# Last pair's third and second-layer expert matrices in four transfers each, with a wait per quarter on TensorE

## The chip, the cores and the metric

The kernel runs on one core of a Trainium2 chip. The metric is the device time of one execution in microseconds (us). One inference step of a small two-layer model for 512 prompt rows and 8 sample rows (one new token each) is one execution.

## The reference

Each of the two layers ends in a mixture of experts over all 520 rows. Cut to what matters here:

```python
yb = silu(xb @ w1[e]) * (xb @ w3[e])   # w1, w3: 1024 x 512, float32
yb = yb @ w2[e]                        # w2: 512 x 1024, float32
y  = sum over a row's two experts of gate * yb
x  = x + y
```

A row is routed to 2 of 32 experts. The matrices of all 32 experts are used in each layer, 3 x 2 MB per expert, so 201 MB per layer are read from HBM whatever the routing says. After layer 0 comes the mixer of layer 1 (means over windows of 2 to 16 rows, then four 256 x 256 maps), after layer 1 the final RMSNorm.

## The kernel before, in words

Everything is float32. Before the experts of layer 0 stand the projections, the attention and the recurrence (the first 400 us or so). The experts of a layer `l` are done in 16 pairs (`PAIRS`): the columns of TensorE are split in two halves of 64 (`CAP`), one expert of the pair in each, so that a pair takes three pair matrices of 4 MB: w1, w3 and w2.

**Slots.** `ring` has six pieces of 16 KB per partition, two per slot; slot 0 is for w1, slot 1 for w3, slot 2 for w2 from pair 4 on (before that four slots rotate). SyncE (SP) issues all weight transfers in one order on one queue: `load(l, i, j, slot, before)` waits until the matrix that lay in the slot has been used (`w1_used`, `h_done`, `y_done`), and issues one transfer that signals `wt_in[slot]`. So a slot's next matrix is requested when PE is done with the last one.

**One pair on PE** (`pair`): wait for w1, `products(0)`; wait for w3, `products(1)` (line 2221, the trace lists 32 matmul records per matrix, in the order of `k`, 0 to 7); transposes of the next pair's rows (`turn`); ACT and DVE form `silu(a) * b` (lines 1187 and 1768); four transposes of it (line 2427), a copy by DVE (line 1773); wait for w2, `results` (line 2247), whose outer loop is over the two 512-column blocks; ACT scales the sum (line 1193) into `yst`, and POOL scatters its rows into `y_rows` in HBM.

**The last pair of a layer** (`last=True`) differs before already. Its w2 comes in two transfers (line 766) with signals `wt_in[2]` and `wt_in[3]`, and `results_by_half` (line 2236) takes `k` as the outer loop and waits for the second half in its middle. Its rows are not scattered. Behind the two transfers SP waits for `w1_used` and for the scatter of pair 14, and then issues `load_results`: for each of the five row tiles (128 rows each, the last has 8) one transfer that gathers the other experts' results from `y_rows` (line 721). For the tiles 0, 1 and 2 DVE adds both gathered parts to `x` (`combine`, lines 1554 and 1557). PE then turns the last pair's rows back to their tokens (`rows_of_last`, lines 2465 and 2466, tile by tile), and DVE adds that (`add_last`, line 1567). Of one thing the order matters here: `rows_of_last(3)` waits until DVE has done `add_last` of tile 0, and `rows_of_last(4)` until that of tile 1, since they take the same PSUM banks. In layer 1 a part of the gathered rows of tiles 3 and 4 is added by PE (line 2465) instead of DVE.

DVE has the order `combine` 0, 1, 2, `add_last` 0 and then, in layer 0, `add_last` 1, the norm of tile 0 for the mixer of layer 1 (lines 1254 and 1255), `add_last` 2, `combine` 3; in layer 1 `combine` 3 and `add_last` 1. Behind `rows_of_last` of layer 0 PE begins the mixer (`mix`, line 2189, and `maps`, line 2210); behind that of layer 1 only norms and stores are left.

`QUARTER` is 1024 words of each of a partition's two 4096-word pieces: two values of `k` in w3, one in w2. The w3 of pair 1 comes in such quarters before the change too (line 754).

Of the kernel before, what the change touches and what calls it, by code (L numbers as in the profile page):

```python
# [7 lines left out]
ALU = mybir.AluOpType  # L24
# [105 lines left out]
def build(nc, a, outs, consts):  # L130
# [11 lines left out]
    with ExitStack() as ctx:  # L142
# [206 lines left out]
        eps_ready = sem("eps_ready")  # L349
# [8 lines left out]
        pick_ready = sem("pick_ready")  # L358
# [7 lines left out]
        rel_ready = sem("rel_ready")  # L366
        brow_done = sem("brow_done")
        brow_ready = sem("brow_ready")
# [19 lines left out]
        SELF_OUT, LOGITS_OUT, PROBS_OUT, PROBS_T_OUT, HEADS_OUT = 1, 2, 3, 5, 7  # L388

        sample_step = sem("sample_step")  # L390
        QUERIES, LOGITS, PROBS_TURNED, ATTENDED, GATES_TURNED, HEADS_TURNED = range(1, 7)
# [4 lines left out]
        lbl_ready = sem("lbl_ready")  # L396
# [23 lines left out]
        s_read = sem("s_read")  # L420
        snorm_ready = sem("snorm_ready")
        osq_summed = sem("osq_summed")
# [9 lines left out]
        late_clear = sem("late_clear")  # L432
# [5 lines left out]
        wr_ready = sem("wr_ready")  # L438
# [17 lines left out]
        hn_stored = [sem(f"hn_stored{l}") for l in range(2)]  # L456
# [15 lines left out]
        wt_in = [sem(f"wt_in{j}") for j in range(4)]  # L472
        w1_used = sem("w1_used")
# [107 lines left out]
        def landed(l, i, j, turned):  # L581

            n = 3 * i + j
            slot = slot_at(i, j) if turned else j
            if slot == 3:
                return 32 * (3 * l + n // 4 + 1) + 16 * l
            in_quarters = 48 * (l + (not turned or n >= 4)) if slot == 0 else 0
            return 16 * ((PAIRS - 1) * l + (n // 4 + 1 if turned else i)) + in_quarters
# [31 lines left out]
        def _(sp):  # L620
# [34 lines left out]
            sp.wait_ge(brow_ready, 2)  # L655
# [67 lines left out]
            for l in range(2):  # L723
# [73 lines left out]
        def _(pool):  # L797
# [10 lines left out]
            pool.wait_ge(brow_ready, 1)  # L808
# [32 lines left out]
            for l in range(2):  # L841
                for p, t in enumerate(TILE_ORDER[l]):
                    n = rows_of(t)
                    pool.wait_ge(hn_ready, TILES * l + p + 1)
                    pool.dma_start(hn_rows[l][t * P:t * P + n, :], hall[0:n, t, :]).then_inc(hn_stored[l], 16)
                pool.wait_ge(hn_stored[l], 16 * TILES)
# [48 lines left out]
        def _(act):  # L895
# [15 lines left out]
            def evacuate(unit, half=0):  # L911
# [14 lines left out]
                elif m == NT:  # L926
                    if PICKED[c]:
                        act.wait_ge(part_picked, PICKED[c])
                    act.wait_ge(pick_ready, 1)
# [4 lines left out]
            act.wait_ge(eps_ready, 1)  # L934
# [16 lines left out]
            act.wait_ge(lbl_ready, 1)  # L951
# [35 lines left out]
            def state_decayed(b):  # L987
                if b == 0:
                    act.wait_ge(s_read, 1)
# [121 lines left out]
            def experts(l):  # L1111
# [30 lines left out]
                if l == 0:  # L1142
                    late = TILE_ORDER[0].index(NT)
                    for u in range(TILES + 1):
# [3 lines left out]
                        if u == late:  # L1148
                            act.wait_ge(wo_done, 2 * u + 2)
                            act.wait_ge(late_clear, 1)  # L1150
# [94 lines left out]
        def _(dve):  # L1245
# [11 lines left out]
            V.memset(eps, EPS).then_inc(eps_ready, 1)  # L1257
# [11 lines left out]
            V.tensor_tensor(lbl, lbl, wide(lbs, [P, 2, HEADS], 1), ALU.subtract).then_inc(lbl_ready, 1)  # L1269

            dve.wait_ge(rel_in, 32)
            V.memset(relx[BUCKETS:BUCKETS + 1, :], 1.0).then_inc(rel_ready, 1)
            dve.wait_ge(rel_ready, 1)
            V.tensor_copy(relrep[0:BUCKETS + 1], wide(relx[0:BUCKETS + 1, :], [BUCKETS + 1, NB, HEADS], 1)).then_inc(rel_ready, 1)
            dve.wait_ge(consts_in, 16)
            V.tensor_reduce(pick, ident.rearrange("p (g c) -> p c g", g=4)[:, 32 - NB:32, :], AX.X, ALU.add).then_inc(pick_ready, 1)
            dve.wait_ge(brow_done, 1)
            V.tensor_copy(brow[0:HEADS], ps[0:HEADS, 4:6, :].rearrange("p a b -> p (a b)")[:, 0:ROWW]).then_inc(brow_ready, 1)
            V.tensor_copy(dbias[0:32], ps[0:32, 6, 0:NDEC]).then_inc(brow_ready, 1)
# [131 lines left out]
            def sample_heads():  # L1411

                dve.wait_ge(s_read, 1)
# [5 lines left out]
            def sample_means():  # L1419
                dve.wait_ge(osq_summed, 1)  # L1420
# [107 lines left out]
            V.memset(partial_late, 0.0).then_inc(late_clear, 1)  # L1528
# [10 lines left out]
            def sample_attended():  # L1539
                dve.wait_ge(sample_step, ATTENDED)  # L1540
                V.tensor_copy(dheads, ps[:, 1, :]).then_inc(decode_step, 2)
# [52 lines left out]
            def experts(l):  # L1594
# [74 lines left out]
                if l == 0:  # L1669
                    for u in range(TILES + 3):  # L1670
# [3 lines left out]
                        if u == 1:  # L1674
# [3 lines left out]
                                            wide(gain_of_router.rearrange("p l k -> p (l k)"), [P, 2 * KC, NG + NE], 2), ALU.mult).then_inc(wr_ready, 1)  # L1678
# [96 lines left out]
                dve.wait_ge(hn_stored[l], 16 * TILES)  # L1775
# [86 lines left out]
        def _(pe):  # L1862
# [41 lines left out]
            def pick_samples(c):  # L1904

                pe.wait_ge(piece_out, upto(UNIT[c, NT]))
                if c == IB:
                    pe.wait_ge(pick_ready, 1)
# [97 lines left out]
            def sample_states(part):  # L2006
# [7 lines left out]
                if part == 3:  # L2014
                    for h in range(HEADS):
                        T.transpose(ps[:, 5, 32 + h * NB:32 + (h + 1) * NB], ib[0:NB, NT, h * DH:(h + 1) * DH], ident[0:NB, 0:NB])
                    T.matmul(ps[:, 5, 64:96], ones, qk.rearrange("p h b -> p (h b)"), start=True, stop=True).then_inc(s_read, 1)

            def sample_squares():
                pe.wait_ge(snorm_ready, 1)  # L2020
                T.matmul(ps[:, 5, 96:128], ones, osq.rearrange("p h b -> p (h b)"), start=True, stop=True).then_inc(osq_summed, 1)
# [62 lines left out]
            for u in range(UNITS):  # L2084
# [7 lines left out]
                elif u == NT:  # L2092
                    pe.wait_ge(rel_ready, 2)
# [3 lines left out]
                    T.matmul(ps[0:32, 6, 0:NDEC], relrep[0:BUCKETS + 1].rearrange("p b h -> p (b h)"), onehot[0:BUCKETS + 1, ROWW:],  # L2097
                             start=True, stop=True).then_inc(brow_done, 1)
                for c in (IB, VA):
                    if u == PICK_AT[c]:  # L2100
                        if c == IB:
                            pe.wait_ge(brow_ready, 2)
# [111 lines left out]
            def products(j, pieces, by_quarter=False):  # L2214
# [3 lines left out]
                for k in range(KC):  # L2218
                    for half, w in enumerate(mats):
# [328 lines left out]
```

## Time and profile before

| what | value |
|---|---|
| time before, median of 3 runs | 1472.81 us (1470.75 to 1473.42) |
| the profiled execution: its span, first to last instruction | 1470.9 us |
| a time of its own beside the span | none is given for it |
| PE matmul busy | 1266.4 us, 86% of the span |
| DVE, ACT, POOL busy | 358.8, 247.0, 83.9 us |
| HBM traffic | 479.75 MB read, 36.56 MB written, 351 GB/s over the span |
| mean granted TensorE clock | 0.952 of full |
| the last pair's products with w3, layer 0 and layer 1, begin at | 875.78 and 1427.58 us |
| the last pair's results, layer 0 and layer 1, begin at | 887.56 and 1439.37 us |

The median stands 1.9 us above the span of the profiled execution. A line such as `L2221` is line 2221 of the kernel before. PE is the matmul side of TensorE, SPq the part of SyncE that issues transfers; in a transfer row the size is that of one transfer and the time is from issue to landing, that is until all of it is there and its signal is complete. The kernel after has the same code some 20 lines higher up.

### The profile page before, as it was taken

The page shows a single profiled execution, that of the slowest core. Times are in us where ns is not written, and L with a number is a line of the kernel's source. Part 1 is how long each engine was busy: PE and PEld are TensorE (multiplying, and loading weights), DVE is VectorE, ACT ScalarE, POOL GpSimd, SP SyncE. Part 2 cuts the span into 40 slices and gives each one's busy share as a digit, 9 for nine tenths or more (in the row PEclk, how much of TensorE's full clock was granted, in tenths as well). Part 3 has the DMA queues.
Part 4 walks back from the last instruction along what each step waited for, and adds up shares of the span by engine and source line. Part 5 has one row for each costly group of instructions (what it writes and reads, how often), then busy time and mean ns, then how long its engine had stood idle before and what let it go on. Part 6 is the DMA issues. An engine that isn't in the chain of part 4 may idle for free.

```text
span 1470.9 us, 14537 instructions
## 1 busy us (share of the span) xinstructions
PE 1266.4 (86%) x5864; PEld 613.9 (42%) x5864; DVE 358.8 (24%) x826; ACT 247.0 (17%) x440; POOL 83.9 (6%) x101
## 2 busy tenths in 40 slices
PE   7999999999999877878878798999977867778787
PEld 3688965644543322322322235853322322322232
DVE  2055487522431000010100007541010000100006
ACT  3243643342200000000000003410000000000002
POOL 1000000000000110000000000000000000000000
PEclk9999999999999988899999999989999999999998
DMA  9435766327479999999999998469999999999994
GB/s 347 103 78 174 219 175 215 106 80 316 201 277 427 426 402 421 427 427 426 428 425 427 426 419 345 194 231 418 426 426 429 426 429 427 427 426 424 428 414 164
DMA packets 75918, 492.94 MB, mean 335 GB/s; under 512 B 16813, under 2 KB 21581, under 8 KB 50774
## 3 DMA queue, kind: packets, MB, share of 16 engines
q1 hardware_dynamic: 59440, 449.35, 74.9%
q0 software_dynamic: 13568, 37.03, 7.5%
q10 hardware_dynamic: 2862, 5.91, 1.2%
q8 instruction: 31, 0.51, 0.1%
q14 instruction: 17, 0.14, 0.0%
HBM read 479.75 MB, written 36.56 MB: 351 GB/s over the span
## 4 chain that ended last, share of the span: by engine, by line
PE 51%; DMA 40%; DVE 5%; ACT 2%; issue 2%; ACTq 0%; SPq 0%; DVEq 0%
DMA ring<-in_moe_w 39%; PE ps L2221 20%; PE ps L1899 5%; PE ps L1892 4%; PE ps L2151 3%; PE ps L2247 3%; PE ps L2321 1%; PE ps L2466 1%; PE ps L2210 1%; PE ps L2236 1%; PE ps L2275 1%; DVE arena L1350 1%; PE ps L1941 1%; PE ps L2189 1%; PE ps L2264 1%
## 5 line engine op out<-in xcount | busy, mean ns | idle before, releaser
L2221 PE MATMUL ps<-ring,arena 128*64 128x512 f32 x1920 | 472.1, 648 | 125.0 <-DMA ring<-in_moe_w 123.2
L2221 PEld LDWEIGHTS ps<-ring,arena 128*64 128x64 f32 x1920 | 150.2, 148 | 440.7 <-issue 269.5
L2247 PE MATMUL ps<-ring,arena 128*64 128x512 f32 x896 | 202.4, 604 | 26.2 <-issue 14.1
L1768 DVE TENSOR_TENSOR arena<-arena,ps 128x512 f32<-128x512 f32 x32 | 22.0, 688 | 784.3 <-ACT arena L1187 784.3
L2247 PEld LDWEIGHTS ps<-ring,arena 128*64 128x64 f32 x896 | 74.5, 139 | 135.0 <-issue 123.1
L1892 PE MATMUL ps<-arena,ring 128*128 128x260 f32 x512 | 117.1, 387 | 0.9 <-ACT arena L921 0.9
L1187 ACT ACTIVATE arena<-ps 128x512 f32<-128x512 f32 x32 | 19.1, 598 | 556.4 <-PE ps L2221 556.4
L1892 PEld LDWEIGHTS ps<-arena,ring 128*128 128x128 f32 x512 | 97.0, 192 | 17.5 <-issue 1.7
L1193 ACT ACTIVATE arena<-ps,arena 128x1024 f32<-128x1024 f32 x32 | 35.7, 1114 | 319.8 <-PE ps L2247 298.9
L1899 PE MATMUL ps<-ring,arena 128*128 128x512 f32 x192 | 86.9, 599 | 0.0
L830 POOL DMA_INDIRECT arena<-hn_rows,arena x30 | 30.7, 1025 | 536.8 <-PE ps L2408 482.9
L2151 PE MATMUL ps<-ring,arena 128*128 128x512 f32 x128 | 56.6, 595 | 0.0
L1899 PEld LDWEIGHTS ps<-ring,arena 128*128 128x128 f32 x192 | 35.7, 192 | 37.9 <-issue 37.4
L836 POOL DMA_INDIRECT y_rows<-arena x30 | 30.4, 1012 | 332.3 <-ACT arena L1193 332.3
L1666 DVE TENSOR_TENSOR arena<-ps,arena 128x1024 f32<-128x1024 f32 x32 | 38.9, 1215 | 1.9 <-PE ps L2330 1.9
L2408 PEld LDWEIGHTS ps<-arena 128*128 128x128 f32 x240 | 28.8, 191 | 24.3 <-issue 24.3
L2427 PE MATMUL ps<-arena 128*128 128x128 f32 x128 | 24.1, 311 | 17.0 <-DVE arena L1768 17.0
L2151 PEld LDWEIGHTS ps<-ring,arena 128*128 128x128 f32 x128 | 23.7, 190 | 26.8 <-issue 26.8
L2408 PE MATMUL ps<-arena 128*128 128x128 f32 x240 | 34.5, 287 | 0.0
L904 ACT ACTIVATE arena<-arena 128x1024 f32<-128x1024 f32 (+1 forms) x25 | 26.3, 1053 | 46.7 <-DVE arena L1592 26.9
L1773 DVE COPY arena<-ps 128x512 f32<-128x512 f32 x32 | 22.1, 692 | 27.0 <-PE ps L2427 27.0
L2221 PE MATMUL ps<-arena 128*64 128x512 f32 x128 | 28.3, 594 | 0.0
(313 smaller groups left out, 1014.0 us busy)
## 6 DMA issues: line engine op xcount, KB each, us to landing
ring<-in_moe_w SPq DMA_DIRECT2D x86, 4096.0 KB, 23.0
arena<-in_moe_w SPq DMA_DIRECT2D x12, 2048.0 KB, 17.4
ring<-in_w_in SPq DMA_DIRECT2D x6, 2048.0 KB, 20.4
y_rows<-c_zero POOLq DMA_DIRECT2D x2, 4160.0 KB, 18.1
ring<-in_moe_w SPq DMA_DIRECT2D x8, 1024.0 KB, 8.1
ring<-in_moe_w SPq DMA_DIRECT2D x4, 2048.0 KB, 18.3
ring<-y_rows SPq DMA_DIRECT2D x8, 1024.0 KB, 15.2
arena<-in_x_prompt SPq DMA_DIRECT2D x8, 512.0 KB, 6.0
```

Source lines behind the costliest of these rows:

```text
L830: pool.indirect_dma_start(out=to, out_offset=None, in_=hn_rows[l][:, :], in_offset=bass.IndirectOffsetOnAxis(ap=slots, axis=0), bounds_che ...
L836: pool.indirect_dma_start(out=rows[:, :], out_offset=bass.IndirectOffsetOnAxis(ap=slots, axis=0), in_=of, in_offset=None, bounds_check=2 * ...
L904: link(nc.scalar.activation(junk_[0:n], x_, ACT.Square, accum_out=r_))
L1193: nc.scalar.activation(yst, ps[:, 5:7, :].rearrange("p a b -> p (a b)"), ACT.Copy, scale=scale).then_inc(y_out, 1)
L1666: V.tensor_tensor(xgT, ps[:, b:b + 2, :].rearrange("p a (k c) -> p (a k) c", k=4), wide(gain_of_rows[:, l, :], [P, KC, 2 * CAP], 2), ALU.m ...
L1892: last = T.matmul(ps[:, piece % 2, 0:HALF], w1v[:, slot, k, m * P:(m + 1) * P], hT[:, k, part * HALF:(part + 1) * HALF], start=(k == 0), s ...
L1899: last = T.matmul(ps[:, piece % 2, :], hT[:, k, m * P:(m + 1) * P], w1v[:, slot, k, :], start=(k == 0), stop=(k == KC - 1))
L2151: last = T.matmul(ps[:, b + c, :], catT[:, k, t * P:(t + 1) * P], w1v[:, WOUT_SLOT + c, k, :], start=(k == 0), stop=(k == KC - 1))
L2221: last = T.matmul(ps[r_, 2 + j, :], xgT[:, k, r_], w[:, k, :], start=(k == 0), stop=(k == KC - 1))
L2247: last = T.matmul(ps[r_, 5 + c, :], hactT[:, k, r_], w[:, k, c * 512:(c + 1) * 512], start=(k == 0), stop=(k == FC - 1))
L2408: last = T.transpose(ps[:, k // 4, (k % 4) * P:(k % 4 + 1) * P], xg[:, k:D:KC], ident)
L2427: t_ = T.transpose(ps[:, 4, k * P:(k + 1) * P], hact[:, k:FE:FC], ident)
```

## The change

Two things are changed in the last pair of each layer. The transfers: w3, which came in one transfer of 4 MB, and w2, which came in two of 2 MB, now come in four of 1 MB each, one behind the other on the same queue, each with a signal of its own (`w3_quarter_in[q]`, `w2_quarter_in[q]`). SP's waits before them are the same two as before (`h_done` and `y_done` of pair 14). PE: `products(1)` waits for quarter `q` of w3 before `k = 2q` instead of once at its head; `results_by_quarter` waits for quarter `k` of w2 before each `k` instead of for a half before `k = 0` and `k = 2`. The order of the matmuls is the same.

```diff
-                for j in range(2):
-                    load(l, PAIRS - 1, j, j, (j, PAIRS * (l + 1) - 1))
-                sp.wait_ge(y_done, PAIRS * (l + 1) - 1)
-                rows = pair_rows("moe_w2", l, PAIRS - 1)
-                for part, signal in ((slice(0, PIECE // 2), wt_in[2]), (slice(PIECE // 2, PIECE), wt_in[3])):
-                    sp.dma_start(ring[:, 4:6, part], rows[:, :, part]).then_inc(signal, 16)
+                load(l, PAIRS - 1, 0, 0, (0, PAIRS * (l + 1) - 1))
+                for name, s, used, signals in (("moe_w3", 2, h_done, w3_quarter_in), ("moe_w2", 4, y_done, w2_quarter_in)):
+                    rows = pair_rows(name, l, PAIRS - 1)
+                    sp.wait_ge(used, PAIRS * (l + 1) - 1)
+                    for q in range(4):
+                        part = slice(q * QUARTER, (q + 1) * QUARTER)
+                        sp.dma_start(ring[:, s:s + 2, part], rows[:, :, part]).then_inc(signals[q], 16)
...
-            def products(j, pieces, by_quarter=False):
+            def products(j, pieces, by_quarter=False, landing=None):
...
                 for k in range(KC):
+                    if landing is not None and k % 2 == 0:
+                        pe.wait_ge(w3_quarter_in[k // 2], landing)
...
-            def results_by_half(pieces, second_half_in):
+            def results_by_quarter(pieces, landing):
...
                 for k in range(FC):
-                    if k == FC // 2:
-                        pe.wait_ge(wt_in[3], second_half_in)
+                    pe.wait_ge(w2_quarter_in[k], landing)
...
                     for j in range(2):
-                        pe.wait_ge(wt_in[slots[j]], landed(l, i, j, turned))
-                        products(j, [weights(slots[j], half) for half in range(2)], first and j == 0).then_inc((w1_used, h_done)[j], 1)
+                        by_landing = last and j == 1
+                        if not by_landing:
+                            pe.wait_ge(wt_in[slots[j]], landed(l, i, j, turned))
+                        products(j, [weights(slots[j], half) for half in range(2)], first and j == 0,
+                                 16 * (l + 1) if by_landing else None).then_inc((w1_used, h_done)[j], 1)
...
-                    pe.wait_ge(wt_in[slots[2]], landed(l, i, 2, turned))
+                    if not last:
+                        pe.wait_ge(wt_in[slots[2]], landed(l, i, 2, turned))
...
-                        results_by_half([weights(slots[2], half) for half in range(2)], 32 * 3 * (l + 1) + 16 * (l + 1)).then_inc(y_done, 1)
+                        results_by_quarter([weights(slots[2], half) for half in range(2)], 16 * (l + 1)).then_inc(y_done, 1)
```

The eight new signals need semaphores, and the change frees eleven by letting early steps share one: `eps_ready`, `lbl_ready`, `rel_ready`, `pick_ready` and `brow_ready`, all raised by DVE in this order, become the seven counts of one `start_step`; `brow_done`, `s_read` and `osq_summed` become counts of PE's `sample_step`; `late_clear` and `wr_ready` become counts of DVE's `decode_step` and `cat_ready`; the two `hn_stored` become one that counts over both layers. The sums in `landed` that say which count means "landed" are adapted to the transfers that left `wt_in[1]`, `wt_in[2]` and `wt_in[3]`. An excerpt:

```diff
-            act.wait_ge(eps_ready, 1)
+            act.wait_ge(start_step, EPS_SET)
...
-                            pe.wait_ge(wr_ready, 1)
+                            pe.wait_ge(cat_ready, 3)
```

## Rows read from the trace of the kernel before

**Rows 1.** The page's part 4, the chain that ended last, by engine.

```profile
PE 51%; DMA 40%; DVE 5%; ACT 2%; issue 2%; ACTq 0%; SPq 0%; DVEq 0%
```

**Rows 2.** Waits: engine, line and releaser: us in total, times, longest us.

```profile
PE ps L2221 <- DMA ring<-in_moe_w: 123.2, 48, 4.0
```

**Rows 3.** Chain at the end of layer 1: start us, us, what.

```profile
1406.45 21.09 DMA ring<-in_moe_w
...
1427.58 8.81 PE ps L2221 x32
```

**Rows 4.** Timeline of PE, end of layer 0: start, us, line, [idle before].

```profile
866.23 7.09 PE L2221 MATMUL ps<-ring,arena 128*64 128x512 f32 x32
875.78 8.78 PE L2221 MATMUL ps<-ring,arena 128*64 128x512 f32 x32 [2.47 <-DMA ring<-in_moe_w]
...
887.56 7.09 PE L2236 MATMUL ps<-ring,arena 128*64 128x512 f32 x32 [0.83 <-issue]
896.03 8.95 PE L2466 MATMUL ps<-arena 128*128 128x512 f32 x20 [1.38 <-ACT arena L1193]
904.91 0.38 PE L2189 MATMUL ps<-arena 128*128 128x128 f32 x1
```

**Rows 5.** Timeline of PE, end of layer 1.

```profile
1417.30 7.09 PE L2221 MATMUL ps<-ring,arena 128*64 128x512 f32 x32 [0.57 <-DMA ring<-in_moe_w]
...
1427.58 8.78 PE L2221 MATMUL ps<-ring,arena 128*64 128x512 f32 x32 [3.19 <-DMA ring<-in_moe_w]
...
1439.37 8.67 PE L2236 MATMUL ps<-ring,arena 128*64 128x512 f32 x32 [0.83 <-issue]
...
1454.69 1.02 PE L2465 MATMUL ps<-ring,arena 128*128 128x512 f32 x2
```

**Rows 6.** Windows: us, busy by engine, then PEclk, DMA share, GB/s.

```profile
600.00:700.00 100.00, 79.55 (x350) 28.96 (x346) 9.98 (x11) 5.74 (x7) 6.09 (x6) 0.93 1.01 427
...
1427.50:1436.40 8.90, 8.78 (x32) 2.61 (x32) 0.00 (x0) 0.00 (x0) 0.00 (x0) 0.81 1.01 401
```

**Rows 7.** Transfers of the last w3, and of w2's halves, layer 1: KB, us to landing.

```profile
ring<-in_moe_w SPq DMA_DIRECT2D x1, 4096.0 KB, 21.1
...
ring<-in_moe_w SPq DMA_DIRECT2D x1, 2048.0 KB, 15.9
...
ring<-in_moe_w SPq DMA_DIRECT2D x1, 2048.0 KB, 20.2
```

**Rows 8.** Packets in 416 to 420, 1436 to 1440 and 977 to 979.5 us.

```profile
DMA packets 421, 1.66 MB, mean 415 GB/s; under 512 B 19, under 2 KB 19, under 8 KB 420
...
DMA packets 419, 1.64 MB, mean 410 GB/s; under 512 B 23, under 2 KB 23, under 8 KB 415
...
DMA packets 176, 0.71 MB, mean 283 GB/s; under 512 B 3, under 2 KB 3, under 8 KB 176
```

**Rows 9.** Timeline of SP's queue: start, us of the issue, line, count.

```profile
1416.61 1.11 SPq L766 DMA_DIRECT2D ring<-in_moe_w  x2
1428.24 2.05 SPq L721 DMA_DIRECT2D ring<-y_rows  x4
1430.34 3.29 SPq L721 DMA_DIRECT2D arena<-y_rows  x1
```

**Rows 10.** Timeline of DVE, end of layer 0.

```profile
888.34 1.23 DVE L1554 TENSOR_TENSOR arena<-ring,arena 128x1024 f32<-128x1024 f32 x1 [0.52 <-DMA ring<-y_rows]
...
894.81 1.23 DVE L1557 TENSOR_TENSOR arena<-ring,arena 128x1024 f32<-128x1024 f32 x1
898.12 1.22 DVE L1567 TENSOR_TENSOR arena<-arena,ps 128x1024 f32<-128x1024 f32 x1 [2.09 <-PE ps L2466]
```

**Rows 11.** Timeline of DVE, end of layer 1.

```profile
1440.13 1.23 DVE L1554 TENSOR_TENSOR arena<-ring,arena 128x1024 f32<-128x1024 f32 x1 [0.87 <-DMA ring<-y_rows]
...
1446.44 1.22 DVE L1557 TENSOR_TENSOR arena<-ring,arena 128x1024 f32<-128x1024 f32 x1
1451.52 1.22 DVE L1567 TENSOR_TENSOR arena<-arena,ps 128x1024 f32<-128x1024 f32 x1 [3.86 <-PE ps L2466]
...
1464.44 1.21 DVE L1567 TENSOR_TENSOR arena<-arena,ps 8x1024 f32<-8x1024 f32 x1 [2.98 <-PE ps L2466]
```

More of the change, by code:

```diff
@@ L387, in build @@
         decode_step = sem("decode_step")
-        SELF_OUT, LOGITS_OUT, PROBS_OUT, PROBS_T_OUT, HEADS_OUT = 1, 2, 3, 5, 7
+        SELF_OUT, LOGITS_OUT, PROBS_OUT, PROBS_T_OUT, LATE_CLEAR, HEADS_OUT = 1, 2, 3, 5, 6, 7
         sample_step = sem("sample_step")
-        QUERIES, LOGITS, PROBS_TURNED, ATTENDED, GATES_TURNED, HEADS_TURNED = range(1, 7)
+        BIASES_SPREAD, STATES_READ, QUERIES, SQUARES_SUMMED, LOGITS, PROBS_TURNED, ATTENDED, GATES_TURNED, HEADS_TURNED = range(1, 10)
+        start_step = sem("start_step")
+        EPS_SET, BOUNDS_SHIFTED, ONE_SET, TABLE_REPEATED, PICK_SET, BIAS_ROWS_OUT, BIAS_COLUMNS_OUT = range(1, 8)
         lb_in = sem("lb_in")
@@ L455, in build @@
         gates_ready = sem("gates_ready")
-        hn_stored = [sem(f"hn_stored{l}") for l in range(2)]
+        hn_stored = sem("hn_stored")
         gat_used = sem("gat_used")
@@ L472, in build @@
         wt_in = [sem(f"wt_in{j}") for j in range(4)]
+        w3_quarter_in = [sem(f"w3_quarter_in{q}") for q in range(4)]
+        w2_quarter_in = [sem(f"w2_quarter_in{q}") for q in range(4)]
         w1_used = sem("w1_used")
@@ L654, in _ @@
             sp.wait_ge(i_stored, 16)
-            sp.wait_ge(brow_ready, 2)
+            sp.wait_ge(start_step, BIAS_COLUMNS_OUT)
             sp.wait_ge(bias_moved, 16)
@@ L1268, in _ @@
             link(V.tensor_tensor(lbs, lbl[:, 0, :], lbl[:, 1, :], ALU.max))
[L1269 removed]
+            V.tensor_tensor(lbl, lbl, wide(lbs, [P, 2, HEADS], 1), ALU.subtract).then_inc(start_step, 1)
             dve.wait_ge(rel_in, 32)
[L1272 to L1274 removed]
+            V.memset(relx[BUCKETS:BUCKETS + 1, :], 1.0).then_inc(start_step, 1)
+            dve.wait_ge(start_step, ONE_SET)
+            V.tensor_copy(relrep[0:BUCKETS + 1], wide(relx[0:BUCKETS + 1, :], [BUCKETS + 1, NB, HEADS], 1)).then_inc(start_step, 1)
             dve.wait_ge(consts_in, 16)
[L1276 to L1279, printed above, removed]
+            V.tensor_reduce(pick, ident.rearrange("p (g c) -> p c g", g=4)[:, 32 - NB:32, :], AX.X, ALU.add).then_inc(start_step, 1)
+            dve.wait_ge(sample_step, BIASES_SPREAD)
+            V.tensor_copy(brow[0:HEADS], ps[0:HEADS, 4:6, :].rearrange("p a b -> p (a b)")[:, 0:ROWW]).then_inc(start_step, 1)
+            V.tensor_copy(dbias[0:32], ps[0:32, 6, 0:NDEC]).then_inc(start_step, 1)
             dve.wait_ge(act_step, LB_EXPED)
@@ L2016, in sample_states @@
                         T.transpose(ps[:, 5, 32 + h * NB:32 + (h + 1) * NB], ib[0:NB, NT, h * DH:(h + 1) * DH], ident[0:NB, 0:NB])
-                    T.matmul(ps[:, 5, 64:96], ones, qk.rearrange("p h b -> p (h b)"), start=True, stop=True).then_inc(s_read, 1)
+                    T.matmul(ps[:, 5, 64:96], ones, qk.rearrange("p h b -> p (h b)"), start=True, stop=True).then_inc(sample_step, 1)
             def sample_squares():
                 pe.wait_ge(snorm_ready, 1)
-                T.matmul(ps[:, 5, 96:128], ones, osq.rearrange("p h b -> p (h b)"), start=True, stop=True).then_inc(osq_summed, 1)
+                T.matmul(ps[:, 5, 96:128], ones, osq.rearrange("p h b -> p (h b)"), start=True, stop=True).then_inc(sample_step, 1)
             def sample_logits():
@@ L2097, in _ @@
                     T.matmul(ps[0:32, 6, 0:NDEC], relrep[0:BUCKETS + 1].rearrange("p b h -> p (b h)"), onehot[0:BUCKETS + 1, ROWW:],
-                             start=True, stop=True).then_inc(brow_done, 1)
+                             start=True, stop=True).then_inc(sample_step, 1)
                 for c in (IB, VA):
```

49 lines of the change are left out of this document (20 added, 29 removed).

## The prediction

> **What bounds the kernel now.** I read the chain that ended last first: it is PE and, for 40% of the span, DMA [rows 1]. The waits say where the two meet: PE waits for expert matrices before its products, 48 times, 123.2 us in all [rows 2]. Inside the pairs nothing can be won by an earlier start of PE, because the queue moves 427 GB/s without a gap [rows 6] and every matrix has to come. The end of a layer is another matter: there the last matrices' work on PE lies behind the last landing, with nothing left to cover it. So I followed the chain through the end of layer 1: the last w3 lands at 1427.5, and all 8.8 us of its products come behind it [rows 3]. The timelines of PE show both ends: PE is done with w1's products at 873.3 and 1424.4 us, sits idle for 2.47 and 3.19 us, and then needs 8.78 us for products that take 7.09 right after other work [rows 4, 5]; in that stretch the granted clock is 0.81, a part of it at the lower of the two levels (1.2 GHz) after the idle time [rows 6].
>
> **w3 in quarters.** PE now needs only the first quarter at its start. Landings in layer 1: w1's products began at 1417.30 on a landing, the last w3 landed at 1406.4 + 21.1 = 1427.5 [rows 5, 7], so 4 MB took 10.2 us on the slowest engine, 2.6 us per quarter. The quarters should be there at about 1420, 1422.5, 1425 and 1427.5, plus what small rows cost (below). PE asks for them at 1424.4 and then each 7.09 / 4 = 1.77 us later, the last at 1429.7, so none is waited for, by 1.8 us or more. Products end at 1424.4 + 7.09 = 1431.5 instead of 1436.4: 4.9 us, 3.2 idle and 1.7 clock. In layer 0 the last quarter is needed at 873.3 + 5.3 = 878.6 and the whole landed at 875.75: products end at 880.4 instead of 884.56, 4.2 us.
>
> **w2 in quarters.** From the end of products to the begin of results ACT, DVE, four transposes and a copy take 3.0 us, unchanged. Results begin at 883.4 and 1434.5. The halves of w2 landed at 1416.6 + 15.9 = 1432.5 and 1417.3 + 20.2 = 1437.5 [rows 7], 10 us behind w3; in layer 0 that is 886. With halves PE, now earlier, would reach the second half at 1438.0, just behind its landing; with quarters the last is asked for at 1439.8 and at 888.7. So w2's quarters are worth nothing by themselves here, at most half a microsecond. Results end at 890.5 instead of 894.65, and at 1441.6 instead of 1448.04 if they go at 7.09 us as in layer 0, not at 8.67 [rows 4, 5].
>
> **What is late next.** PE would be 4.2 and 6.5 us earlier at `rows_of_last`, but DVE gates it there. DVE starts `combine` on a landing of the gather, at 888.34 and 1440.13, and ends tile 2 at 896.04 and 1447.66 [rows 10, 11]. These times hang on the queue, not on PE, and stay. Today DVE then waits for PE, 2.09 and 3.86 us. In the changed kernel it goes straight on with `add_last(0)`, ready at 897.26 and 1448.88, and only then may PE do tile 3. PE is through tiles 0 to 2 at 891.9 + 5.3 = 897.2 and 1443.0 + 5.3 = 1448.3, both just before DVE. Let d be the delay of the gather.
> - Layer 0: tiles 3 and 4 are 8 of the 20 records of 8.95 us, 3.6 us, so the mixer starts at 897.26 + 3.6 + d = 900.85 + d instead of 904.91: **4.1 - d**. The mixer behind it is a chain of PE, ACT and DVE, released by this one; it moves as a whole, and layer 1's transfers with it, each of which waits for a use.
> - Layer 1: tile 3 starts at 1448.88 + d instead of 1454.69: **5.8 - d**. From there to DVE's last sum at 1464.44 and the final store PE works without a pause, as now.
>
> **The size of d.** Rows of 16 KB (w3) and 8 KB (w2) become rows of 4 KB. Where nearly all packets were of 4 KB and the queue was full, 415 and 410 GB/s were moved, against 427 with the large rows [rows 6, 8]: 4.19 MB in 10.2 instead of 9.8 us, 0.4 us for w3. For w2 I take nothing: while its halves and the gather moved, the rate was 401 already [rows 6]. The bounds are 0, and, where quarters came one by one with a queue that had run low, 283 GB/s [rows 8], which would make d 9.4. I take 0.4, since here the queue is full. The Trainium skill ("DMA: Bandwidth & Descriptors", section "Bandwidth") has a measurement that speaks against this change: 1 MB in one transfer moves at 341 GB/s, 16 MB at 425. By its 341 d would be an estimated 4.3 us, and the sum 1.3 us.
>
> **Costs that I put at nothing.** SP issues 8 instead of 3 transfers per layer, five more at 0.4 to 0.8 us each. It has 9 us between the w3 and the w2 issues and 11 from 1416.61 to the gather at 1428.24, for which it waits anyway [rows 9]. One issue there took 3.29 us, as if held until room was made. Were SP held so for several quarters, the gather would be issued later, but the queue would by then be full of what holds it; uncovered it would go into d. The added waits on PE, 5 per layer, are met when they come: the half's wait in layer 0 left 7.09 us for 32 records [rows 4]. The shared semaphores only renumber steps that one engine raises in one order, so no wait ends later.
>
> **Sum.** 4.1 + 5.8 - 2 x 0.4 = 9.1 us. The profiled span of 1470.9 becomes 1461.8. The median shown is 1.9 above that span, 1472.81; I predict 1472.8 - 9.1 = **1463.7 us**.
>
> **The rivals.**
> - Clock. If results or products run with an idle spell's low clock (layer 1's results did today, 1.6 us [rows 5]), layer 0 loses 1.2 (of 1.6, 0.4 lie under DVE) and layer 1 0.6: gain 7.3, 1465.5 us. For it: clock changes depend on where the idle time falls. Against: products now follow w1's without a gap. Chance 0.12.
> - A gather later by 2 us, for small rows or SP's held issues: 9.9 - 4 = 5.9, 1466.9 us. Chance 0.10.
> - The quarters land together at the end, because the 16 engines are far apart: then w3's products start as before and 0.4 later, twice: 1473.6 us. Against it the halves of w2, issued 0.7 us apart, landed 5 us apart [rows 7]. Chance 0.05.
> - The quarters move midway between rows 8's 410 and 283 GB/s, at 346: w3 and w2 take 12.1 us each instead of 10.2 and 10, d is 4.0, the gain 1.9, 1470.9 us. Against: rows of 4 KB moved 410 GB/s in transfers of 1 MB [rows 8]. Chance 0.03. The Trainium skill's figure above, from the same page and section, is about this case.
> - Slower: quarters of 4 KB rows at the 283 GB/s of rows 8. w3 and w2 would take 14.8 us each, the gather lands 9.4 us later, and DVE's `combine` ends behind today's begin of `add_last`: 9.9 - 18.8 = -8.9, 1481.7 us. It turns into a loss from d = 5 on, that is at under some 330 GB/s. Against: that row is of transfers issued one by one as PE released them. Chance 0.03.
>
> **How the numbers follow.** My case has 0.67. A measurement of this kernel can tell 0.2% or 2.9 us from no change. The case itself and the first two rivals are faster by more, 0.89; together-landing and the midway rate are within, 0.08; the last is slower, 0.03. The range: d = 0 gives 1462.9, less the 1.3 us by which runs differ, 1461.5; d = 2 with the slow clock gives 1468.7. The cases beyond it hold 0.11.
>
> **What would show it.** In PE's timeline of after: w1's and w3's products of the last pair as one block of 64 records and about 14.1 us in both layers, with no wait for DMA between; results begin about 4 and 5 us earlier against the gather's issue. On DVE: no idle time, or under 0.5 us, between line 1557 and the first `add_last`; the first `combine` at most 0.5 us later against the issue of w2. On PE a pause of about a microsecond or less before tile 3, released by DVE. If idle time before w3's quarters remains, the landings are not one by one; if `combine` is later by 2 us or more, the small rows or SP's issues are to blame.

## The result, and the profile after

| | before | changed |
|---|---|---|
| median of 5 runs, us | 1472.81 (1470.70 to 1473.42) | 1465.18 (1464.05 to 1466.29) |
| ratio, 95% interval | | 0.9945 [0.9923, 0.9966] |
| span of the profiled execution, us | 1470.9 | 1463.0 |
| mean granted TensorE clock | 0.952 | 0.958 |

The change gains 7.6 us, 0.55%, clear of the 0.2% named in the prediction. It said 9.1 us. The lines of the kernel after stand lower by 14 to 19: L2204 is `products` (before L2221), L2218 `results_by_quarter`, L2451 and L2452 `rows_of_last`, L1535 and L1538 `combine`, L1548 `add_last`.

First the page of the changed kernel: its span, the busy times (of each engine: us, share of the span, count of instructions), and the chain by engine, which answers to [rows 1].

```profile
span 1463.0 us, 14558 instructions
...
PE 1258.2 (86%) x5864; PEld 612.3 (42%) x5864; DVE 358.4 (24%) x826; ACT 246.8 (17%) x440; POOL 83.7 (6%) x101
...
PE 50%; DMA 39%; DVE 6%; ACT 2%; issue 2%; ACTq 0%; SPq 0%; DVEq 0%; POOLq 0%
```

PE's busy time fell by 8.2 us for the same 5864 records: none was removed, some ran at a higher clock. Not all of this is the edit's: cut at the begins of PE that the table below uses, the two ends have 1.9 and 3.8 us less, the mixer has 2.2 us more, and the 15 pairs of layer 1, which nothing in the edit touches, have 4.2 us less and are only 0.5 us shorter. The waits for expert matrices before products, against [rows 2] (us in total, times, longest):

```profile
PE ps L2204 <- DMA ring<-in_moe_w: 119.3, 46, 4.5
```

Two waits are gone, one per layer. PE's timeline at both ends of a layer, against [rows 4, 5] (start, us, engine, line, what, records, [idle before <- releaser]):

```profile
865.82 13.96 PE L2204 MATMUL ps<-ring,arena 128*64 128x512 f32 x64
881.19 0.75 PE L2412 MATMUL ps<-arena 128*128 128x128 f32 x4 [1.42 <-DVE arena L1749]
882.72 7.09 PE L2218 MATMUL ps<-ring,arena 128*64 128x512 f32 x32 [0.78 <-DVE arena L1754]
891.20 8.95 PE L2452 MATMUL ps<-arena 128*128 128x512 f32 x20 [1.39 <-ACT arena L1174]
900.08 2.05 PE L2170 MATMUL ps<-arena 128*128 128x128 f32 x16
...
914.98 1.97 PE L2257 MATMUL ps<-arena 128*128 128x36 f32 x16 [1.11 <-ACT arena L1101]
...
917.68 0.47 PE L2170 MATMUL ps<-arena 128*128 128x128 f32 x2
...
918.23 0.78 PE L2170 MATMUL ps<-arena 128*128 128x128 f32 x2
...
1415.13 13.95 PE L2204 MATMUL ps<-ring,arena 128*64 128x512 f32 x64 [0.58 <-DMA ring<-in_moe_w]
1430.50 0.74 PE L2412 MATMUL ps<-arena 128*128 128x128 f32 x4 [1.41 <-DVE arena L1749]
1432.03 7.09 PE L2218 MATMUL ps<-ring,arena 128*64 128x512 f32 x32 [0.78 <-DVE arena L1754]
1440.52 5.42 PE L2452 MATMUL ps<-arena 128*128 128x512 f32 x12 [1.41 <-ACT arena L1174]
1447.29 1.13 PE L2451 MATMUL ps<-ring,arena 128*128 128x512 f32 x2 [1.35 <-DVE arena L1548]
```

Products of w1 and w3 are now one block of 64 records in both layers, where [rows 4, 5] had 7.09 us, an idle spell of 2.47 or 3.19 us and 8.78 us. No quarter is waited for. In layer 1 the results take 7.09 instead of 8.67 us. Only one wait is new: 1.35 us before tile 3 of layer 1, for DVE's `add_last`. DVE's own timeline, against [rows 10, 11]:

```profile
887.21 1.23 DVE L1535 TENSOR_TENSOR arena<-ring,arena 128x1024 f32<-128x1024 f32 x1 [4.18 <-DMA ring<-y_rows]
...
893.81 1.22 DVE L1538 TENSOR_TENSOR arena<-ring,arena 128x1024 f32<-128x1024 f32 x1
894.95 2.35 DVE L1548 TENSOR_TENSOR arena<-arena,ps 128x1024 f32<-128x1024 f32 x2
...
1438.62 1.23 DVE L1535 TENSOR_TENSOR arena<-ring,arena 128x1024 f32<-128x1024 f32 x1 [6.65 <-DMA ring<-y_rows]
...
1444.87 1.22 DVE L1538 TENSOR_TENSOR arena<-ring,arena 128x1024 f32<-128x1024 f32 x1
1446.02 1.21 DVE L1548 TENSOR_TENSOR arena<-arena,ps 128x1024 f32<-128x1024 f32 x1
...
1456.55 1.21 DVE L1548 TENSOR_TENSOR arena<-arena,ps 8x1024 f32<-8x1024 f32 x1 [0.61 <-PE ps L2452]
```

The idle time before the first `add_last` (2.09 and 3.86 us before) is gone: DVE goes straight on. To see where the 7.9 us between the two spans lie, I cut both executions at four begins of PE: the last pair's products of layer 0, the first record of the mixer, the first expert product of layer 1, the last pair's products of layer 1.

| stretch, us | before | changed | gain |
|---|---|---|---|
| up to the last pair of layer 0 | 866.23 | 865.82 | 0.4 |
| end of layer 0, to the mixer | 38.68 | 34.26 | 4.4 |
| mixer of layer 1, to its experts | 66.52 | 69.66 | -3.1 |
| 15 pairs of layer 1 | 445.87 | 445.39 | 0.5 |
| end of layer 1, to the end of the span | 53.60 | 47.87 | 5.7 |

So both ends gave 10.1 us together, and the mixer took 3.1 back. The mixer's work is the same; the windows (us, busy by engine, PEclk, DMA share, GB/s) show its clock, first of the changed kernel, then of the kernel before.

```profile
910.20:920.20 10.00, 8.89 (x58) 8.26 (x58) 6.81 (x24) 4.16 (x8) 0.00 (x0) 0.89 0.92 371
920.20:930.20 10.00, 10.00 (x57) 9.52 (x57) 3.23 (x8) 5.21 (x9) 0.59 (x1) 0.77 0.26 108
940.20:950.20 10.00, 10.00 (x44) 5.79 (x44) 3.22 (x21) 3.78 (x7) 0.54 (x1) 0.66 0.45 161
```

```profile
915.00:925.00 10.00, 8.89 (x68) 8.26 (x67) 6.81 (x24) 4.20 (x8) 0.00 (x0) 1.00 0.89 351
925.00:935.00 10.00, 10.00 (x76) 9.28 (x76) 5.87 (x24) 5.81 (x10) 0.59 (x1) 1.00 0.30 123
945.00:955.00 10.00, 10.00 (x56) 5.55 (x54) 4.59 (x21) 4.83 (x8) 0.55 (x1) 0.87 0.66 236
```

PE is busy all the time in the last two windows of each, yet from 920 on the changed kernel gets through 57 records where the one before gets through 76: a part of it at the lower level of 1.2 GHz. In the timeline above the fall stands between two records of the same line: 0.47 us at 917.68, 0.78 us at 918.23. The mixer before the change has slow stretches too, but later ones: a clock of 0.87 from 945 on, and 0.75 in its last 6.5 us, where the changed one has 0.97 in its last 9.7 us. The 3.1 us are what is left of the two.

### The profile page after: what moved, and what is told of

Same layout as the page of the kernel before. It is cut to its first block, busy times and chain, and to the rows that moved or that the text cites. A ratio compares the mean times of both kernels' runs of the same rounds, so it can differ in the third digit from the quotient of the medians.

```text
span 1463.0 us, 14558 instructions
## 1 busy us (share of the span) xinstructions
PE 1258.2 (86%) x5864; PEld 612.3 (42%) x5864; DVE 358.4 (24%) x826; ACT 246.8 (17%) x440; POOL 83.7 (6%) x101
## 4 chain that ended last, share of the span: by engine, by line
PE 50%; DMA 39%; DVE 6%; ACT 2%; issue 2%; ACTq 0%; SPq 0%; DVEq 0%; POOLq 0%
DMA ring<-in_moe_w 36%; PE ps L2204 20%; PE ps L1880 5%; PE ps L2229 4%; PE ps L1873 4%; PE ps L2132 3%; PE ps L2191 1%; PE ps L2303 1%; DMA ring<-y_rows 1%; PE ps L2257 1%; DVE arena L1331 1%; PE ps L2452 1%; PE ps L2170 1%; PE ps L2246 1%; PE ps L1922 1%
## 5 line engine op out<-in xcount | busy, mean ns | idle before, releaser
L2204 PE MATMUL ps<-ring,arena 128*64 128x512 f32 x1920 | 464.8, 640 | 121.3 <-DMA ring<-in_moe_w 119.3
L2204 PEld LDWEIGHTS ps<-ring,arena 128*64 128x64 f32 x1920 | 149.1, 146 | 430.8 <-issue 265.1
L1873 PEld LDWEIGHTS ps<-arena,ring 128*128 128x128 f32 x512 | 95.9, 190 | 17.1 <-issue 1.7
L1880 PEld LDWEIGHTS ps<-ring,arena 128*128 128x128 f32 x192 | 35.3, 190 | 37.3 <-issue 36.8
L2204 PE MATMUL ps<-arena 128*64 128x512 f32 x128 | 28.3, 594 | 0.0
## 6 DMA issues: line engine op xcount, KB each, us to landing
y_rows<-c_zero POOLq DMA_DIRECT2D x2, 4160.0 KB, 17.7
```

Of the source, the lines that this page charges most:

```text
L1873: last = T.matmul(ps[:, piece % 2, 0:HALF], w1v[:, slot, k, m * P:(m + 1) * P], hT[:, k, part * HALF:(part + 1) * HALF], start=(k == 0), s ...
L1880: last = T.matmul(ps[:, piece % 2, :], hT[:, k, m * P:(m + 1) * P], w1v[:, slot, k, :], start=(k == 0), stop=(k == KC - 1))
L2204: last = T.matmul(ps[r_, 2 + j, :], xgT[:, k, r_], w[:, k, :], start=(k == 0), stop=(k == KC - 1))
```

## The experiments

The kernels ran in three groups of four, each group beside the kernel before on the same chip (its medians there: 1474.65, 1473.82 and 1472.57 us). A ratio is against those runs, with its 95% interval. Where the number of parts is varied, the kernel has this edit and a table of the parts per layer; where a table says (4, 4), (4, 4), it is the changed kernel:

```diff
-                    for q in range(4):
-                        part = slice(q * QUARTER, (q + 1) * QUARTER)
+                    for q in range(parts):
+                        part = slice(q * PIECE // parts, (q + 1) * PIECE // parts)
...
-                    if landing is not None and k % 2 == 0:
+                    if landing is not None and k % (KC // W3_PARTS[landing]) == 0:
...
+                    if k % (FC // W2_PARTS[landing]) == 0:
```

**w3 alone, w2 alone.**

```diff
+        W3_PARTS, W2_PARTS = (4, 4), (2, 2)
```

> w3 of the last pairs in quarters, w2 in halves as before. Theory A (all of the gain is w3's, w2's second half is there when PE gets to it): like the changed kernel, 1465.2 us, within 1 us; PE's results of the last pair take 7.1 us in one piece, or wait up to 0.5 us in the middle. Rival B (w2's quarters carry a part): 1.5 us or more slower than the changed kernel, with a wait for DMA inside the results of layer 1.

```diff
+        W3_PARTS, W2_PARTS = (1, 1), (4, 4)
```

> w3 of the last pairs whole, w2 in quarters. Theory A: no gain, 1472.8 us within 1.5 us; PE waits 2.5 and 3.2 us before w3's products as in the kernel before. Rival B: faster than before by 1.5 us or more.

Measured: w3 alone 1467.46 us, ratio 0.9962 [0.9942, 0.9982]; w2 alone 1470.93 us, 0.9990 [0.9968, 1.0012]. The gain comes with w3's quarters; w2's have none that can be measured. In w2_only PE waits for the whole w3 as before, 2.36 us in layer 0 and 3.43 in layer 1, and its results in layer 0 take 7.09 us, as they did. In w3_only, where PE comes early to a w2 in halves, the results of layer 1 take 7.38 us, 0.3 more than with quarters; its results of layer 0 took 8.55 us, which was not expected.

**One layer at a time.**

```diff
+        W3_PARTS, W2_PARTS = (4, 1), (4, 2)
```

> Quarters in layer 0 alone. Theory A with a clock that gives back part of layer 0's gain in the mixer: the mixer of layer 1 (first mixer matmul to the first expert product of layer 1) takes some 69.7 us as in the changed kernel instead of 66.5, and the time falls by 2.2 us only, to 1470.6. Rival C (that loss was an accident of one profiled run): the mixer takes 66.5 us and the time falls by 4.8 to 1468.

```diff
+        W3_PARTS, W2_PARTS = (1, 4), (2, 4)
```

> Quarters in layer 1 alone. Theory A: the mixer is untouched, 66.5 us, and the end of layer 1 gives 5.7 us: 1467.1 us. Rival C (the mixer's loss is an accident): the mixer takes anything between 66 and 70 us. The two gains, of layer 0 alone and of layer 1 alone, add up to the 7.6 us of both within 1 us by theory A.

Measured: layer 0 alone 1471.70 us, ratio 0.9980 [0.9961, 1.0000]; layer 1 alone 1469.90 us, 0.9977 [0.9958, 0.9996]. Each gives about half of the gain, and 0.20% and 0.23% add up to 0.43%, the size of the whole within the intervals. The mixer took 68.5 us in the profile of layer 0 alone and 66.5 in that of layer 1 alone, as if its loss went with layer 0's quarters; the repeats below say otherwise. The spans of single executions would mislead here (1475.6 and 1465.8 us): layer0_only's was longer by 3.1 us in the pairs of layer 1, which it does not touch, and its own last pair ran at a low clock:

```profile
1431.29 9.85 PE L2206 MATMUL ps<-ring,arena 128*64 128x512 f32 x32 [3.44 <-DMA ring<-in_moe_w]
```

**The changed kernel again.** Unchanged, in the second group and in the third, to have its scatter beside its neighbours'.

> The changed kernel as it is, on the same chip as the next three. Theory A: 7 to 8 us under the kernel before; 64 products of the last pair in one block of 14.0 us; DVE's first sum of the gather 21.4 to 23.5 us after the begin of w1's products. Whether the mixer between the layers takes 66.5 us here or 69.7 as in the first profile tells whether its 3.1 us belong to this kernel (theory A2: the clock follows the earlier start) or to that run (rival C).

> The changed kernel on the same chip as the three before. 7 to 8 us under the kernel before by theory A. The mixer takes either some 66 or some 69.5 us; a third profile of the same kernel.

Measured: 1467.85 us, ratio 0.9956 [0.9936, 0.9976], and 1465.93 us, 0.9955 [0.9931, 0.9979]. The mixer took 65.48 and 66.62 us in these two, against 69.66 in the first profile: the same kernel has it either way. The results of layer 0 took 8.78 and 8.59 us, where the first profile had 7.09.

**The split without the use of it.** The transfers stay four, and PE waits for all of w3 at the head of its products.

```diff
-                    if landing is not None and k % 2 == 0:
-                        pe.wait_ge(w3_quarter_in[k // 2], landing)
+                    if landing is not None and k == 0:
+                        for q in range(4):
+                            pe.wait_ge(w3_quarter_in[q], landing)
```

> The transfers in quarters as in the changed kernel, but PE waits for all four quarters of w3 before its first product. Theory A (the gain is the wait per quarter, splitting by itself is worth nothing): within 1.5 us of the kernel before, idle 2.5 to 3.5 us before w3's products. Rival D (splitting the transfers is what helps, since the scatter of pair 14 then lands after 7.2 instead of 9.5 us and the gather is issued 2.3 us sooner): 2 us or more faster than before.

Measured: 1474.68 us, ratio 1.0004 [0.9984, 1.0024]: the whole gain is gone. Its timeline of PE in both layers:

```profile
870.10 7.09 PE L2205 MATMUL ps<-ring,arena 128*64 128x512 f32 x32
880.20 8.59 PE L2205 MATMUL ps<-ring,arena 128*64 128x512 f32 x32 [3.01 <-DMA ring<-in_moe_w]
...
1423.67 7.09 PE L2205 MATMUL ps<-ring,arena 128*64 128x512 f32 x32 [2.27 <-DMA ring<-in_moe_w]
1434.50 9.62 PE L2205 MATMUL ps<-ring,arena 128*64 128x512 f32 x32 [3.75 <-DMA ring<-in_moe_w]
```

It also measures what small rows cost: all of w3 is there 10.10 and 10.83 us after the begin of w1's products, against 9.55 and 10.28 before [rows 4, 5], so 0.55 us later in both; against all profiles with w3 in one transfer, which have 9.45 to 9.64 and 10.28 to 10.53, it is 0.3 to 0.65 us.

**Two parts instead of four.**

```diff
+        W3_PARTS, W2_PARTS = (2, 2), (2, 2)
```

> w3 and w2 of the last pairs in two halves each. By the landings, the first half of w3 is there 5 us before the whole, so at about 1422.4, before PE asks at 1424.4, and the second is asked for at 1427.9, after it landed at 1427.5. Theory A: like the changed kernel within 1 us, the 64 products in one block or with a wait of up to 0.5 us. Rival: halves are too coarse, 2 us or more slower, with a wait between record 48 and 49.

Measured: 1468.29 us, ratio 0.9960 [0.9941, 0.9979]. The first line of each layer in its timeline of PE, and what follows it in layer 0:

```profile
866.45 10.52 PE L2206 MATMUL ps<-ring,arena 128*64 128x512 f32 x48 [0.49 <-DMA ring<-in_moe_w]
877.16 3.65 PE L2206 MATMUL ps<-ring,arena 128*64 128x512 f32 x16 [0.19 <-DMA ring<-in_moe_w]
...
1417.27 14.10 PE L2206 MATMUL ps<-ring,arena 128*64 128x512 f32 x64 [0.58 <-DMA ring<-in_moe_w]
```

PE waits 0.19 us for the second half of w3 in layer 0, and for nothing in layer 1, where the block is 0.15 us longer than with quarters. In the same group the changed kernel had 0.9956: the runs can't tell two parts from four.

**DVE's order at the end of layer 1.** Since DVE became what is waited for, I let it do the first `add_last` before the third `combine`.

```diff
-            for t in range(3):
-                combine(1, t)
+            combine(1, 0)
+            combine(1, 1)
             for u in range(TILES + 1):
                 if u < TILES:
                     add_last(1, u)
-                if u + 3 < NT:
-                    combine(1, u + 3)
+                if u + 2 < NT:
+                    combine(1, u + 2)
```

> The changed kernel, and in layer 1 DVE does the last sum of tile 0 before the gathered sums of tile 2 (and of tile 1 before tile 3's). Theory A (DVE's order holds PE at tile 3 for 1.35 us): that pause goes, the end of layer 1 is 1.2 us shorter, 1 us under the changed kernel. Rival: the gather's landing of tile 3 is what holds PE, then the pause stays and nothing is won.

Measured: 1468.92 us, ratio 0.9965 [0.9944, 0.9987], no better than the changed kernel in the same group. PE's wait for DVE went, and another stood behind it:

```profile
1450.21 1.10 PE L2451 MATMUL ps<-ring,arena 128*128 128x512 f32 x2 [0.63 <-DMA ring<-y_rows]
```

Tile 3 adds gathered rows, and they land only then; from the begin of w1's products it is 31.43 us instead of 32.16. So theory and rival both hold a part: the pause for DVE went, tile 3 begins 0.7 us sooner, and there its landing holds PE. The end of the layer took 48.92 us, the changed kernel's 47.87, 49.11 and 50.07.

**Work for PE in its idle spells.** My theory for the 3.1 us in the mixer was that the clock fell because PE had been idle (1.11 us before L2257, above). Matmuls of the identity, whose result is overwritten, fill the spells: in the last pair behind its products and its transposes, in the mixer before that line, or in both.

```diff
+                            if u == 1:
+                                for _ in range(4):
+                                    T.matmul(ps[:, 3, 0:P], ident, ident, start=True, stop=True)
...
+                    else:
+                        for _ in range(5):
+                            T.matmul(ps[:, 0, 0:P], ident, ident, start=True, stop=True)
...
+                    if last:
+                        for _ in range(3):
+                            T.matmul(ps[:, 0, 0:P], ident, ident, start=True, stop=True)
```

This is filled_both; filled_mixer has the first of the three pieces, filled_pair the other two.

> The changed kernel with matmuls of no use in three idle spells of PE: 5 and 3 small ones (128x128) before and behind the last pair's transposes, and 4 before the mixer's first router product of layer 1, into unused PSUM banks. Theory E (the idle spells let the clock fall, and that takes part of the gain back): last pair's results at 7.1 us in both layers, the mixer at 66.6 us or less in place of up to 69.7, 1.5 to 4 us under the changed kernel beside it. Rival F (the mixer's narrow matmuls let the clock fall, whatever the spell of 1.1 us before them; or the clock's fall is of the chip, not of the kernel): no gain, the mixer at 69 us in some profile.

> Matmuls of no use in the last pair's two idle spells alone. Theory E: results of layer 0 take 7.1 us instead of the 8.5 or so that four of six profiles with quarters in layer 0 showed, the time from w1's products to the mixer is 34.3 us instead of 35.8; 1 us under the changed kernel. Rival F: the results take 8.5 us here too.

> Four matmuls of no use in the mixer's 1.1 us wait alone. Theory E: the mixer takes 66.6 us or less. Rival F: it takes 68.5 to 69.7 us as in four of the six profiles with quarters in layer 0.

Measured: both 1467.16 us, ratio 0.9960 [0.9940, 0.9981]; the pair 1467.73, 0.9962 [0.9944, 0.9980]; the mixer 1466.04, 0.9950 [0.9929, 0.9970]; the changed kernel beside them 0.9955. None is better than that. The mixer took 66.52, 69.66 and 69.68 us in the three. The last one is the case that speaks against the theory:

```profile
917.18 1.06 PE L2371 MATMUL ps<-arena 128*128 128x128 f32 x8
918.46 1.97 PE L2257 MATMUL ps<-arena 128*128 128x36 f32 x16 [0.22 <-ACT arena L1101]
...
920.71 0.47 PE L2170 MATMUL ps<-arena 128*128 128x128 f32 x2
...
921.87 0.78 PE L2170 MATMUL ps<-arena 128*128 128x128 f32 x2
```

The idle time before L2257 is down to 0.22 us, and the clock falls some 3 us behind it all the same. So the spell is not needed for the fall. In filled_both, with the same 0.22 us there, the clock did not fall in this stretch. The theory fell for this spell. In the pair, the results took 7.09 us in both layers of all three kernels, but they did so in the changed kernel's first profile as well, so that this proves nothing.

## Why the prediction was right, and where it was not

**w3 in quarters: right.** Products end 13.96 and 13.95 us after w1's begin; before it was 18.33 and 19.06 us [rows 4, 5]. That is 4.4 and 5.1 us earlier, where the step said 4.2 and 4.9. In all ten profiles in which a layer 0 used parts of w3, that block took 13.95 us or, with halves, 14.36 us: the low clock that followed the idle spell is gone with the spell. Of the eight such spells in the profiles where PE waited for all of w3 (2.36 to 3.75 us), seven were followed by 8.59 to 9.85 us for these products and one by 7.09 (w2_only, layer 1), so in a layer the 1.7 us of clock are likely but not sure. split_wait_all shows that it is the earlier start, not the transfers, that gives this.

**w2 in quarters: right.** Put at nothing, at most half a microsecond; w2_only measured 0.9990 [0.9968, 1.0012], and halves of w2 with quarters of w3 do as well as all quarters. These times can't resolve half a microsecond; the one trace of it is the 0.3 us in w3_only's results.

**What is late next: right in layer 1, and in layer 0 where the gather comes late.** In layer 1 tile 3 was put at 1448.88 + 0.4, that is 31.98 us behind w1's begin. It began at 32.16, released by DVE after a pause of 1.35 us, and at 32.02 and 32.15 in the two repeats. In layer 0 DVE was expected to be the gate too. In the first profile its first sum came earlier than I put it, and PE ran through all 20 records without a pause, so that the results' end set the mixer's begin: 34.26 us behind w1's products, against 35.02 predicted. Where the gather came later and the results ran at full clock, DVE was the gate, as in halves, filled_both and sums_in_turn:

```profile
898.53 3.80 PE L2456 MATMUL ps<-arena 128*128 128x512 f32 x8 [0.86 <-DVE arena L1549]
```

```profile
901.58 3.80 PE L2461 MATMUL ps<-arena 128*128 128x512 f32 x8 [0.84 <-DVE arena L1548]
```

```profile
897.12 3.80 PE L2452 MATMUL ps<-arena 128*128 128x512 f32 x8 [1.78 <-DVE arena L1548]
```

In all three the mixer begins 5.0 us behind the begin of the first `add_last`. In the repeats the results ran at a low clock (8.78 and 8.59 us) and the mixer began at 35.96 and 35.76 us behind w1's products, again without a pause of PE. By those 5.0 us DVE alone would have let it begin 0.6 and 0.4 us sooner, and the rest of the 1.7 and 1.5 us against the first profile is the later gather. The rival "Clock" was thus true of layer 0 in some executions, but by this estimate at about half a microsecond and not 1.2; its other half, layer 1's results at a low clock, appeared in none of the three (7.09 us).

Over all profiles the end of layer 0 took 38.7 us on average in the four kernels in which PE waited for all of w3 there, and 35.4 in the ten with parts: 3.4 us where the step gave 3.7. The end of layer 1 took 52.8 us in the four that waited for all of w3 there and 49.1 in the ten with parts: 3.7 where the step gave 5.4. Two things made the term too large. One is the clock that the kernel before happened to have: in w2_only w3's products and the results ran at full clock without parts, and its end took 49.86 us, while the profile that I worked from had 53.60. Tile 3 began 36.8 us behind w1's begin on average in the four and 32.0 in the ten, 4.9 us sooner and not 5.4. The other is "PE works without a pause, as now", which leaves out the clock: from tile 3's begin to the end of the span it took 15.6 to 16.3 us in the four, and with parts 15.7 or 15.8 in three profiles and 17.1 to 17.9 in the other seven, 1.2 us more on average. The difference lies in the last small records, here of the first profile after and of after_third:

```profile
1453.68 1.88 PE L2451 MATMUL ps<-arena 8*8 8x512 f32 x4
```

```profile
1452.47 3.25 PE L2451 MATMUL ps<-arena 8*8 8x512 f32 x4
```

What lets the clock fall there, no run shows.

**The size of d: about right, with a sign in layer 0 that changes.** I took 0.4 us for w3's small rows, and split_wait_all shows 0.3 to 0.65. But the gather is not only behind w3. Its first sum stands 22.11 and 22.83 us behind w1's products before [rows 4, 5, 10, 11] and 21.39 and 23.49 us after: d was -0.7 in layer 0 and +0.7 in layer 1. In the repeats it was +0.6 and +0.8 in layer 0 and +0.5 and +0.6 in layer 1, so layer 0's gather was early only in some executions (in three of the eight profiles in which layer 0 used quarters of both matrices). Two effects stand against each other that I had not seen, a gather issued sooner and a gather that takes longer; the last section has them. The bound of 9.4 us was far off, and with it the midway rate and the loss: from 1404 to 1430 us the queue moved 409 GB/s, with nearly all packets small. The Trainium skill's rate of 341 GB/s for a transfer of 1 MB ("DMA: Bandwidth & Descriptors", section "Bandwidth"), which spoke against the change, is not borne out in this full queue. (The estimate of d from it comes to 4.4 us, not 4.3, and so the sum by it to 1.1.) The packets of that stretch:

```profile
DMA packets 2353, 10.63 MB, mean 409 GB/s; under 512 B 223, under 2 KB 223, under 8 KB 2197
```

**Costs at nothing: right for PE's waits, not separated for SP.** The issues of the gather took SP 4.98 and 6.02 us for four, where it was 2.05 in [rows 9]. The first of them was out sooner all the same, but the fourth was issued 14.7 us behind w1's begin in layer 1 instead of 13.0. It stood in a full queue, yet in sums_in_turn it is a landing of the gather that PE waits for before tile 3, so whether SP's issues cost something there or only the load of the queue does, no run separates. SP's queue in layer 1:

```profile
1404.26 15.85 SPq L747 DMA_DIRECT2D ring<-in_moe_w  x8
1423.81 6.02 SPq L701 DMA_DIRECT2D ring<-y_rows  x4
1429.87 2.15 SPq L701 DMA_DIRECT2D arena<-y_rows  x1
```

**The step that failed** is "it moves as a whole", said of the mixer behind layer 0; the same fault is in "PE works without a pause, as now" behind tile 3 of layer 1. The mixer began 4.4 us earlier and lost 3.1 us of that in the profiled execution. Its times fall in two groups, 65.5 to 66.6 us and 68.5 to 69.7 us. The kernels without parts in layer 0 had the short one in all four profiles, those with parts the long one in six of ten. That looks like a cost of the earlier start, but the changed kernel itself had 69.66, 65.48 and 66.62 us, and four profiles are few. Nor is the mixer's time independent of what comes before: of the four profiles with parts in which layer 0's results ran at a low clock (8.52 to 8.78 us), three had a short mixer, and of the six with results at 7.1 us, five had a long one. End and mixer together took 104.9 us on average in the four and 103.6 in the ten, a gain of 1.4 us where the step gave 3.7. What makes the clock fall there stays open: in filled_mixer it fell with only 0.22 us left of the idle spell before L2257, and no run here gives another cause. With a term of some 2 us for it (the mixer's average is 68.2 us in the ten and 66.2 in the four) and the averages of the two ends, 3.4 and 3.7, the sum of 9.1 comes down to 5.1; the medians of the timed runs differ by 7.6, 6.0 and 6.6 us, within some 3 us each way, so that the mixer's loss may well be less than my few profiles show. In short: the mechanism was right, and the sum 1.5 to 3 us too large; the mixer's clock and layer 1's, which the step and the term left out, are more than enough to make up for that. The three profiles of the changed kernel differ in where they are slow, yet both ends and the mixer together took 151.8, 150.6 and 152.5 us in them, against 158.8 before, 157.2 in split_wait_all and 154.7 in w2_only.

## What to carry over

Where a transfer is the last of its kind and its consumer is short of work, let the consumer take it in parts: the gain is the idle time and, where one followed it, the slow clock. Two parts were enough here, and a split that is waited for as a whole gains nothing. Look at what is released next before adding it up: the first engine that the earlier end runs into, and, on TensorE, whether the work behind is held by the clock rather than by its inputs.

## What the runs showed of the hardware that was not expected

**A scatter lands sooner beside small packets.** POOL scatters pair 14's rows into `y_rows` while w3 and w2 of the last pair are under way, and SP waits for it before it issues the gather. The transfers issued from 1404 to 1430 us (queue, operation, count, KB each, us from issue to landing), of the kernel before, of the changed one, and of w3_only:

```profile
ring<-y_rows SPq DMA_DIRECT2D x4, 1024.0 KB, 15.0
y_rows<-arena POOLq DMA_INDIRECT x1, 9.5
```

```profile
ring<-y_rows SPq DMA_DIRECT2D x4, 1024.0 KB, 17.7
...
y_rows<-arena POOLq DMA_INDIRECT x1, 7.2
```

```profile
y_rows<-arena POOLq DMA_INDIRECT x1, 8.7
```

The scatter takes 9.7 and 9.5 us (layer 0 and 1) before, 7.3 and 7.2 with both matrices in quarters, 8.6 and 8.7 with only w3 in quarters, 8.6 and 8.5 with halves of both, 9.4 and 10.6 with only w2 in quarters; split_wait_all has 7.3 and 7.5 without any earlier use. layer0_only has 7.3 in layer 0 and 10.6 in layer 1, layer1_only 9.8 and 7.2: it goes with the packets beside it, not with the run. In the two repeats and the three filled kernels it was 6.9 to 7.5 in both layers. The Trainium skill says that an engine takes turns between its queues packet by packet ("DMA: Bandwidth & Descriptors", section "Queues, rings and completion order"); the times agree with that, since a packet of a small queue would then wait for one of 4 KB instead of one of 16 or 8 KB. That this is the cause is argued, not shown: the number of transfers changed together with their packets. It brings little here: SP issues the gather 2.3 us sooner in layer 1, but it stands behind the same matrices, and its transfers take 17.7 instead of 15.0 us.

**The clock falls under a PE that is busy.** It fell inside a stretch of small matmuls in which PE had no idle time (917.68 to 918.23 us in the changed kernel, 920.71 to 921.87 in filled_mixer); in the two repeats of the changed kernel it did not fall there.

**The stretches far from the edit scatter by as much as its gain.** The 15 pairs of layer 1, the same in all kernels, took 445.3 to 446.2 us in nine profiles and 448.2 to 449.3 in five, of edited and unedited kernels alike. A span of one execution can't tell a gain of 3 us; the stretches by themselves can.
